# Two transformer-like blocks in one kernel: the first product stage reordered, and the second block's projection and scan joined in one block

## The reference, cut to what matters

```python
# first block
h = rms_norm(x, g_norm1) * (1.0 + scale1) + shift1          # scale1, shift1 from silu(c) @ w_mod
x_lru, z_lru, q, k, v = split(h @ w_in)
xc = conv4(x_lru) + conv_b                                   # then two gated recurrences, attention
x = x + gate1 * (concatenate([y_lru, y_att]) @ w_out)
x = x + gate2 * expert_choice_ffn(rms_norm(x) ...)           # 16 experts
# second block
h = layer_norm(x, ln_emb_g, ln_emb_b)
xs, z, bm, cm, dt_raw, glu, cgate = split(h @ w_in_2)
xs, bm, cm = silu(conv4([xs, bm, cm]));  dt = softplus(dt_raw + dt_bias);  a = -exp(a_log)
# the scan: 8 chunks of 128 rows, 2 groups of 8 heads
a_cs = cumsum(dt * a) within the chunk
ldec = exp(where(causal, a_cs[l] - a_cs[s], -inf))
y = (C B^T * ldec) @ (xs * dt)  +  (C @ state) * exp(a_cs)
state = state * exp(a_cs[-1]) + B^T @ (xs * dt * exp(a_cs[-1] - a_cs))
y_ssm = rms_norm((y + d_skip * xs) * silu(z)) * ssm_norm_g
u = conv31(glu[:, :1024] * sigmoid(glu[:, 1024:]))
y_conf = silu(layer_norm(u, conf_ln_g, conf_ln_b)) * silu(cgate)
out = [y_ssm, y_conf] @ w_out_2 + b_out;  two more layer norms and a gated sum follow
```

## Time and profile before

| | |
|---|---|
| Median of three runs | 2200.85 us (2200.64 to 2201.06) |
| The profiled execution, in all | 2202.2 us |
| Its span | 2200.5 us |
| TensorE busy | 2074.6 us, 94% of the span, 9840 matmuls |
| VectorE busy | 1685.9 us, 77% |
| ScalarE busy | 1064.4 us, 48% |
| GpSimd busy | 215.9 us, 10% |
| Mean DMA rate | 173 GB/s |

### The profile page before, as it was taken

The page is one execution under the profiler, slowest core; times in us unless marked ns, Lnnn a source line. Parts: engine busy times, 40 slices in busy tenths (PEclk is TensorE's granted clock), DMA queues, the critical chain, the costliest instruction groups (busy, mean ns, idle before and its releaser), DMA issues. The chain is left out here.

```text
span 2200.5 us, 24911 instructions
## 1 busy us (share of the span) xinstructions
PE 2074.6 (94%) x9840; PEld 1605.9 (73%) x9840; DVE 1685.9 (77%) x1717; ACT 1064.4 (48%) x1215; POOL 215.9 (10%) x168
## 2 busy tenths in 40 slices
PE   6999998999997999999999759999999988899998
PEld 4767844777865788888888647888888864588876
DVE  4575247896557899999999678999999966864776
ACT  4388134894235677777777423112132157523043
POOL 0200010000000011110110210000000004224040
PEclk9999997999988999999999969999999998999999
DMA  7411161002368999999999751111122234343121
GB/s 268 125 39 39 39 233 70 1 1 88 125 259 342 346 385 398 397 393 401 393 398 395 215 156 41 58 58 66 50 87 96 96 138 168 130 157 115 39 77 58
DMA packets 130030, 381.71 MB, mean 173 GB/s; under 512 B 9563, under 2 KB 21115, under 8 KB 129936
## 3 DMA queue, kind: packets, MB, share of 16 engines
q1 hardware_dynamic: 116144, 340.41, 40.8%
q0 software_dynamic: 7568, 23.09, 4.2%
q10 hardware_dynamic: 6224, 16.93, 1.9%
HBM read 337.28 MB, written 43.06 MB: 173 GB/s over the span
## 5 line engine op out<-in xcount | busy, mean ns | idle before, releaser
L2307 DVE SCALAR_TENSOR_TENSOR arena<-arena,vecs 128x1023 f32<-128x1023 f32 (+14 forms) x240 | 304.4, 1268 | 7.1
L2011 DVE TENSOR_TENSOR w_low<-W,w_high 128x2048 fp32r<-128x2048 f32 x96 | 216.9, 2286 | 34.2 <-ACT w_high L1932 34.2
L2011 DVE TENSOR_TENSOR w_low<-arena,w_high 128x2048 fp32r<-128x2048 f32 x96 | 218.4, 2289 | 19.3 <-ACT w_high L1932 19.3
L1784 PE MATMUL Q<-hT_high,w_high 128*128 128x512 f32 (+1 forms) x736 | 229.4, 391 | 1.3 <-PEq L1804 1.3
L1784 PE MATMUL Q<-hT_low,w_high 128*128 128x512 f32 (+1 forms) x720 | 224.7, 390 | 0.0
L1932 ACT ACTIVATE w_high<-arena 128x2048 fp32r<-128x2048 f32 x96 | 184.1, 1919 | 74.2 <-PE Q L1850 74.2
L1784 PE MATMUL Q<-hT_high,ring_low 128*128 128x512 f32 x704 | 219.5, 389 | 0.0
L1932 ACT ACTIVATE w_high<-W 128x2048 fp32r<-128x2048 f32 x96 | 184.0, 1919 | 69.7 <-PE Q L1850 65.7
L1797 ACT ACTIVATE w_high<-W 128x1024 fp32r<-128x1024 f32 x44 | 46.5, 1058 | 256.1 <-PE Q L1784 243.0
L1850 PE MATMUL Q<-w_high,x_high 128*128 128x512 f32 x512 | 160.9, 396 | 2.4 <-DVE x_low L2014 2.4
L1784 PEld LDWEIGHTS Q<-hT_high,w_high 128*128 128x128 f32 (+1 forms) x736 | 135.3, 184 | 33.3 <-issue 1.8
(11 more groups left out here) (457 smaller groups left out, 4146.7 us busy)
## 6 DMA issues: line engine op xcount, KB each, us to landing
arena<-in_w_dram SPq DMA_DIRECT2D x48, 2048.0 KB, 11.7
W<-in_w_dram SPq DMA_DIRECT2D x48, 2048.0 KB, 12.5
W<-in_w_mod_dram SPq DMA_DIRECT2D x12, 2048.0 KB, 13.4
W<-in_w_in_dram SPq DMA_DIRECT2D x12, 2048.0 KB, 9.0
W<-in_w_out_dram SPq DMA_DIRECT2D x6, 2048.0 KB, 11.0
spill<-arena ACTq DMA_DIRECT2D x24, 512.0 KB, 2.6
W<-in_w_in_dram SPq DMA_DIRECT2D x8, 1024.0 KB, 8.7
arena<-spill SPq DMA_DIRECT2D x3, 2048.0 KB, 12.3
```

What stands on the lines that cost most here:

```text
L1784: ins = nc.tensor.matmul(Q[rows, 2 * pair_of(n) + half, :], w[:, k], x[:, k, HALF * half:HALF * half + HALF], start=k == 0 and w is high a ...
L2011: nc.vector.tensor_tensor(wl[:], chunk_src(r, j), wh[:].bitcast(F32), ALU.subtract).then_inc(low_v, 1)
L2307: ins = nc.vector.scalar_tensor_tensor(conf[:, i, j:], u[:, 0:S - j], w, conf[:, i, j:], ALU.mult, ALU.add)
```

## The change

Four parts.

1. First stage. TensorE begins with feature 0 of block 0 in the order high x high, low weights x high, high x low (`first_of_all`), and each part waits only for what it reads. ScalarE rounds the weights of features 0 and 1 ahead of h. VectorE's list is interleaved anew, the mod products 2 and 3 and the turns move between the groups of `early`, convolution 0 goes ahead of the second copy, and features 5 to 7 are rounded after three finished products, not four.
2. The 12 small loads of the second block move from the end of the experts to the block of the first output projection, at the head of GpSimd's list. The weights of dt get a tile of their own.
3. The scan has no block of its own any more. `chunk(0)` stands within the last product z7, behind its second k; `conf_silu` stands ahead of the read of z6; `scan_begin` (growth factors, turned B, decays 0 and 1) stands ahead of the read of z7; `inputs(0)` and `chunk_cb(0)` stand between VectorE's gate multiplications. x comes in four loads, the first into a tile of its own and sent after the variance's sums.
4. Buffers are placed anew for that (state, turned, cb, the sums of step 1 and others), the state's two PSUM banks change places, and the first two updates of the state are copies in place of a multiplication and a sum.

```diff
+                def first_of_all():
+                    _, high, low = feature_parts(0)
+                    parts = ((high, h1_high), (low, h1_high), (high, h1_low))
+                    pe.wait_ge(in_high_ready, 1)
+                    pe.wait_ge(h1_high_ready, 1)
+                    for p, (w, h) in enumerate(parts):
+                        if p == 1:
+                            pe.wait_ge(in_low_ready, 1)
+                        if p == 2:
+                            pe.wait_ge(h1_low_ready, 1)
+                        for half in range(2):
+                            nc.tensor.matmul(Q[:, half, :], w[:, 0], h[:, 0, HALF * half:HALF * half + HALF],
+                                             start=p == 0, stop=False)
...
-                for k in range(KD // 2):
-                    pe.wait_ge(h1_low_ready, k + 1)
-                    for f in range(3):
-                        early(f, k)
-                        if k == KD // 2 - 1 and f < 2:
-                            turn_part(2 + f)
-                        if (k, f) in ((KD // 2 - 2, 2), (KD // 2 - 1, 0)):
-                            mod_product(pe, unit(pe, 2 if f == 2 else 3), 6)
+                first_of_all()
+                early(1, 0)
+                early(2, 0)
+                mod_product(pe, unit(pe, 2), 6)
+                pe.wait_ge(h1_low_ready, 2)
+                for f in range(3):
+                    early(f, 1)
+                turn_part(2)
+                mod_product(pe, unit(pe, 3), 6)
+                pe.wait_ge(h1_low_ready, 3)
+                for f in range(3):
+                    early(f, 2)
+                turn_part(3)
+                pe.wait_ge(h1_low_ready, 4)
+                for f in range(3):
+                    early(f, 3)
...
+                in_first(0)
+                in_first(1)
                 h_first(0)
-                for f in range(3):
-                    in_first(f)
+                in_first(2)
...
                 send_sums(sync, 0)
+                for j in range(2):
+                    sync.wait_ge(stage_out[j], 16 * KD)
+                sync.wait_ge(in2_mm, place["var", 0] + 1)
+                send_xs(0)
+                sync.wait_ge(in2_mm, place["z", 6] + 1)
+                send_sums(sync, 1)
+                sums_behind(3)
                 sync.wait_ge(in2_mm, len(order))
-                for n, cols_n in enumerate((slice(0, P), slice(P, 4 * P), slice(4 * P, S))):
-                    sync.dma_start(xs[:, :, cols_n], spill[12:20, :, cols_n].rearrange("m p n -> p m n"))\
-                        .then_inc(xs_in[n], 16)
+                send_xs(1)
+                send_sums(sync, 2)
+                send_xs(2)
+                for i in range(4, STEPS):
+                    sums_behind(i)
+                    if i == 5:
+                        send_xs(3)
...
+                        if (kind, m) == ("z", 7) and k == SPREAD_AT:
+                            chunk(0)
                         ins = product2(pe, n, i, k, (1,) if i < AHEAD else (0, 1))
...
-                    if what == ("z", 7):
+                    if what == ("z", 6):
                         for k in range(KD):
                             conf_silu(k)
+                    if what == ("z", 7):
+                        scan_begin()
...
                 for k in range(KD):
+                    if k == 3:
+                        inputs(0)
+                        chunk_cb(0)
                     dve.wait_ge(conf_act, k + 1)
```

More of the change, by code:

```diff
@@ L2182, in spread, with chunk @@
                     return ins
+                def chunk(c):
+                    cols_c = slice(P * c, P * c + P)
+                    if c:
+                        pe.wait_ge(xw_ready, 2 * c)
+                        pe.wait_ge(turned_ready, c)
+                        pe.wait_ge(cb_ready, c)
+                    else:
+                        pe.wait_ge(in2_s, s_level["var", 0])
+                        pe.wait_ge(conf_scaled, KD)
+                    if c in (0, 1, 2, 4):
+                        pe.wait_ge(xs_in[(0, 1, 2, 2, 3)[c]], 16)
+                    for k in range(KD):
+                        nc.tensor.transpose(Q[:, k // 4, P * (k % 4):P * (k % 4) + P],
+                                            xs[:, k, cols_c] if c else xs_first[:, k], ident[:])
+                    for g in range(2):
+                        nc.tensor.transpose(Q[:, 2, P * g:P * g + P], bc_conv[:, g, cols_c], ident[:])
+                    for g in range(2):
+                        ins = nc.tensor.matmul(Q[:, 2, 2 * P + P * g:3 * P + P * g], bc_conv[:, g, cols_c],
+                                               bc_conv[:, 2 + g, cols_c], start=True, stop=True)
+                    ins.then_inc(chunk_mm, 1)
@@ L2217, in _ @@
                             spread(place["var", 1]).then_inc(in2_mm, 1)
+                        if (kind, m) == ("z", 7) and k == SPREAD_AT:
+                            chunk(0)
                         ins = product2(pe, n, i, k, (1,) if i < AHEAD else (0, 1))
                     ins.then_inc(in2_mm, 1)
+                for i in range(STEPS):
+                    if i % 2 and i + 1 < STEPS:
+                        chunk(i // 2 + 1)
+                    outputs(i)
+                    if 2 <= i + 1 < STEPS:
+                        carried(i + 1)
             @block.scalar
@@ L2296, in _ @@
                         squares()
+                for i in range(2, STEPS):
+                    c, g = divmod(i, 2)
+                    decays(i)
+                    if g == 0:
+                        read_turned(c)
+                    if i == 2:
+                        act.wait_ge(cg_used, KD)
+                        conf_high_part(0)
+                    if g:
+                        conf_high_part(c)
                 act.wait_ge(stage_out[0], 16 * (len(staged) // 2))
@@ L2345, in long_taps, with inputs @@
                         taps_done[0] = q + 1
+                def inputs(i):
+                    c, g = divmod(i, 2)
+                    dve.wait_ge(chunk_mm, c + 1)
+                    if i == 1:
+                        dve.wait_ge(stage_out[0], 16 * (len(staged) // 2))
+                    if i >= 3:
+                        dve.wait_ge(y_mm, i - 2)
+                        dve.wait_ge(st_mm, i - 2)
+                    xg = Q[:, g, :].rearrange("p (h n) -> p h n", h=HPG)
+                    for j, part in enumerate((0, 2)):
+                        dst = x_dt[i % 3][:, HALF * j:HALF * j + HALF].rearrange("p (h n) -> p h n", h=HPG)
+                        per_head = segment_cols(part, i).rearrange("p (h o) -> p h o", o=1)
+                        ins = nc.vector.tensor_tensor(dst, xg, per_head.broadcast_to((P, HPG, DK)), ALU.mult)
+                    ins.then_inc(xw_ready, 1)
@@ new lines, in evac_y @@
+                def evac_y(i):
+                    c, g = divmod(i, 2)
+                    dve.wait_ge(y_mm, i + 1)
+                    for m in range(4):
+                        b, cols_c = 4 * g + m, slice(P * c, P * c + P)
+                        x_b = xs[:, b, cols_c] if c else xs_first[:, b]
+                        ins = nc.vector.scalar_tensor_tensor(y_ssm[:, b, cols_c], x_b, skip_col[:, b:b + 1],
+                                                             Q[:, Y_BANKS[i % 2], P * m:P * m + P], ALU.mult, ALU.add)
+                    ins.then_inc(y_out, 1)
```

342 lines of the change are left out of this document (150 added, 192 removed).

## The result

The changed kernel took 2184.46 us, the median of four runs (2180.36 to 2185.76), beside 2200.95 for the kernel before (2200.64 to 2201.22). The ratio of its runs to those of the kernel before is 0.9913, 95% interval 0.9901 to 0.9926, or 19 us. The forecast was 2179.2 with a range of 2174 to 2188. A second series, of six runs, gave 2182.68 (2177.88 to 2188.59) against 2201.39 before, ratio 0.9918 (0.9903 to 0.9933). So it is faster by 16 to 19 us, where 21.6 was forecast. One run of the kernel before in a later series, 4228.8 us, is slow and left out of every ratio.

What follows compares the result with a forecast made beforehand. TensorE sets the time, handing over step by step with VectorE in the scan. First stage 6.2, small loads 2.5 and scan 12.9 sum to 21.6 us, for a median of 2179.2 us, range 2174 to 2188.

Steps and rivals of the forecast that it cites:

- First stage: Start of the kernel: TensorE starts earlier and its second pause goes, 6.2 us gained, ends 3 and 7.5.
- The second pause: TensorE's 2.14 us idle in the middle of the first stage; to vanish, with TensorE going on at 57.4, not 61.77.
- The 1.8 us for the low clock behind it: First stage, after the second pause: 9 matmuls at 1.2 GHz return to full clock, 1.8 us of the 6.2.
- Small loads, old place: After the experts: without twelve small transfers VectorE's 2.48 us wait for a token row goes, 2.5 us, ends 0 and 4.
- Small loads, new place: First output projection: x's load ends at 541.0 despite the small packets, last moment 541.5; no loss, up to 5 us.
- Rival B: First output projection: small packets jam the load of x, TensorE stands up to 5 us; 2184.2, chance 15%.
- Scan: Opening of the scan: both idle times of TensorE go, step 2's outputs 12.9 us earlier, ends 14.5 and 5.
- the landing: Opening of the scan: step 2's sums land at 1815.5, behind x's second columns, after the product's end at 1809.4.
- The room of 1.9 us for step 1's inputs: Opening of the scan: VectorE has them at 1812.9; chunk 1, behind x at 1814.8, asks first, 1.9 us later.
- Rival C: Opening of the scan: step 2's sums land late, at 1823.7, the sum shrinks by 8.2 to 13.4; 2187.4, chance 12%.
- E: Last product before the scan: chunk 0 inside it waits for x or scaling and holds TensorE; 2202 or more, 3%.
- D: First stage: its gain is lost to ScalarE's table loads and chains or an earlier clock fall; 2185.4, chance 10%.

Runs made afterwards that it cites:

- the part alone: Only the first-stage reordering put on the kernel before: 2195.76 us, ratio 0.9967 (0.9956 to 0.9978).
- this part alone: Only the 12 small loads moved to the first output projection, on the kernel before: 2200.55 us, ratio 0.9994 (0.9983 to 1.0004).
- the parts' medians: Kernel before with one part each: first stage 2195.76 us, small loads 2200.55, scan with its buffers 2190.39; together 21.6 below the kernel before.

## Why the prediction was right in the mechanism and 3 to 5 us off in the size

**First stage.** Forecast 6.2, measured 6.3 and 5.3 in the two profiles of the changed kernel, 4.6 in that of the part alone, 7.0 by the part's median; 5.3 between the middles of all profiles with the new and the old order. The start was forecast for 33.1 and was at 33.17, but 1.1 to 1.4 us later in the three profiles in which the weights landed late, which the forecast did not allow for. The second pause is gone. The 1.8 us for the low clock behind it were read from one execution: a low stretch stood there in one of the three profiles with the pause, and the stage ended 1.0 us later in it than in the two others. So that the first profile gives 6.3 for 6.2 is in part luck.

**Small loads, old place.** Forecast 2.5, measured 2.5 to 2.6 in every kernel with that part. Held.

**Small loads, new place.** The step failed: "I take nothing". The forecast saw the margin, 541.0 against a last moment of 541.5, and took the jam of the old place, 8.5 us, for the jam at the new one. Small packets lay there beside the last 1.3 MB of SyncE's loads, and x came 3.8 us after VectorE was ready for it, at 542.8 on the scale of the kernel before where 541.0 was forecast. Measured 0.7 to 1.5 us lost in the eight profiles with the loads sent at once (1.26 with this part alone), none in the three with the loads held. Rival B came about, at a seventh to a third of its price. A margin of half a microsecond under an estimate with an error of several is no margin; the likely value there was a loss of one or two.

**Scan.** Forecast 12.9, measured 12.0 in the first profile. (By the same landmarks the second gives 10.4; 1.6 of the difference lie inside the projection, where its clock was low for 3.4 us near the start, and C is the same.) Chunk 0 in the product cost 1.46, not 1.7, and had no wait. The link that sets step 2 was named rightly, its sums behind x's second columns, and the chain from there to the outputs was forecast at 8.12 and measured at 8.24, within 0.01 in all six profiles with x sent first. The term that was mis-sized is the landing: 6.1 us behind the product (x's 5.4 and 1.3 for 512 KB at full rate are 6.7, and the forecast took less because the gate loads would be over), measured 7.0. (Other loads and the store of z7 are in flight at the same time; that these make the difference was not tried.) With x's second columns behind them the sums landed at 4.6. The room of 1.9 us for step 1's inputs was wrong too: forecast for 3.5 behind the product, they were done at 6.0, and chunk 1 waited for VectorE and not for x. Rival C (landing as late as 13.2) did not come about.

VectorE's three gate multiplications took 5.66 us beside GpSimd, 3.84 with GpSimd's instruction cut short. The rule of the Trainium skill (SBUF — State Buffer, section SBUF: two separate sides), that whoever comes second at the shared port pair is blocked for the whole instruction, agrees with this, at a size of 1.8 us here. The forecast gave it up to 1 us of the sum. No run shows a part of the sum lost to it: with the instruction cut short C stayed at 15.5.

**Behind the scan.** No term stood there, and in the first profile 3.3 us went. This is the largest part of the miss in that execution; in the other it was 0.7 us. The forecast took one profiled execution as if its low stretches were fixed: it moved everything behind the scan rigidly. The kernel before has the same chance in it, 2198.5 to 2208.36 in 19 runs of one series, though its four first runs agreed within 0.6 us and hid that. By the table of landmarks even a stretch with no change in it, the attention between 296.79 and 516.32, gained 1.2 us in one execution and 3.9 in the other. What belongs to the change, summed over its places in the first profile, is 6.3 - 1.5 + 2.6 + 12.0 = 19.4 us: the forecast's 21.6 less 1.5 for the new place and 0.9 for the landing, and 0.2 more from the rest. With the 5.3 of all profiles for the first stage it is 18.4. The ratios of the two series say 19.1 and 18.0.

**The sides.** E, a wait for x inside the last product, did not come; the row of chunk 0 has no wait. Nor did D: the part alone kept its gain by the median.

What stays open is the size of chunk 0's place, and why the medians of the whole change lie 3 to 5 us above the sum of the parts' medians; with series of four to eight runs of kernels that spread by 5 to 10 us both can be chance.

## What to carry to other kernels

A stretch of TensorE without a gap passes a gain on to the end, and it can be summed by places; but the places where it idles or makes thin matmuls hold low-clock stretches of another length in each execution, so read them in more than one profile before counting single microseconds. Small packets are best sent when nothing urgent is in flight: moving them to a place with half a microsecond to spare moves the jam too. A start that is moved up to a transfer's landing takes over the spread of that landing. When one wait is removed, list what lands next in the order of issue; here it was one load, and then the one behind it.

## What the runs showed of the hardware

The packets of the 12 small loads cost by their number: 235 of them with less than 0.01 MB held 71.3% of the DMA engines for 10 us. A low clock followed 32 matmuls of one column (3.6 to 4.1 us without a wait on either side) in each profile with them on end, for 3.4 or 6.8 us, and did not with the same matmuls spread among full ones. In 13.5 us at 1.2 GHz at the scan's end TensorE was busy for 9.55. Of two loads asked for together by SyncE the one asked for first landed first: the sums 4.6 to 5.9 us behind the product when first, 7.0 to 8.5 when second. The 2 MB of weights at the start took 20.0 to 20.1 us to land in eleven profiles and 21.4 to 21.7 in three. Runs of one kernel differed by up to 10.7 us, and the mean granted clock goes with it (0.972 and 0.966 at the two ends).
